# Two-layer encoder with routed experts on one core: the last gate matrix of each layer brought by eleven unequal transfers

## The reference, cut to what matters

```python
def block_fn(args):
    rows, e = args
    xb = x_pad[rows]
    h = jax.nn.silu(xb @ w_gate[e]) * (xb @ w_up[e])
    return h @ w_down[e]
```

## Time and profile before

| what | value |
|---|---|
| median of three runs | 1161.56 us (1160.43 to 1163.86) |
| the profiled execution's own time | 1162.22 us |
| its span, first to last instruction | 1160.4 us |
| time around the span | 1.8 us |
| busy share of the span: PE, PE weight loads, DVE, ACT, POOL | 76%, 44%, 20%, 15%, 4% |
| moved by DMA | 439.26 MB, 379 GB/s over the span |
| chain that ended last | PE 48%, DMA 45% |
| mean TensorE clock granted | 0.88 |

### The profile page before, as it was taken

How to read it: one execution, slowest core, us unless ns; L and a number is a source line. 1 busy time by engine, 2 the same in 40 slices (tenths; PEclk the granted TensorE clock), 3 DMA queues, 4 the chain that set the end, 5 groups by cost and what they waited for, 6 DMA issues and landing times.

```text
span 1160.4 us, 20228 instructions
## 1 busy us (share of the span) xinstructions
PE 879.7 (76%) x9135; PEld 510.6 (44%) x9135; DVE 237.3 (20%) x784; ACT 169.1 (15%) x459; POOL 41.5 (4%) x46
## 2 busy tenths in 40 slices
PE   9999995666576757566899999987575676666666
PEld 4454663434344434343544556644242443433343
DVE  2351421111012111110234435211110111111111
ACT  1141310101011101000224232211010110101011
POOL 1651000000000000000000000000000000000000
PEclk9999998879888887888999998988787787878789
DMA  9992999999999999999973258999999999999996
GB/s 347 336 324 99 380 428 425 429 425 429 426 428 426 426 429 424 429 426 425 393 292 118 100 227 353 383 424 429 426 428 426 426 428 425 430 425 427 426 426 271
DMA packets 46261, 439.26 MB, mean 379 GB/s; under 512 B 4640, under 2 KB 5888, under 8 KB 21344
## 3 DMA queue, kind: packets, MB, share of 16 engines
q1 hardware_dynamic: 43632, 433.96, 89.7%
q0 software_dynamic: 1088, 2.97, 1.1%
q10 hardware_dynamic: 1456, 1.04, 0.3%
HBM read 436.91 MB, written 1.05 MB: 377 GB/s over the span
## 4 chain that ended last, share of the span: by engine, by line
PE 48%; DMA 45%; another core or an unknown queue 2%; DVE 2%; ACT 1%; issue 1%; SPq 0%; POOL 0%; DVEq 0%
DMA mem<-in_moe_w_up 44%; PE psum L1311 43%; PE psum L1449 3%; PE psum L1441 1%; PE psum L1332 1%; DMA mem<-in_ev_w_in 1%; SPq L440 0%; DVE mem L962 0%; PE psum L1318 0%; ACT mem L645 0%; DVE mem L1112 0%; DVE mem L1108 0%; PE psum L1610 0%; PE psum L1376 0%
## 5 line engine op out<-in xcount | busy, mean ns | idle before, releaser
L1311 PE MATMUL psum<-mem 128*32 128x256 f32 (+3 forms) x7114 | 671.7, 438 | 258.8 <-DMA mem<-in_moe_w_up 226.2
L1311 PEld LDWEIGHTS psum<-mem 128*32 128x32 f32 (+2 forms) x7114 | 346.8, 132 | 554.9 <-issue 459.9
L1011 DVE TENSOR_TENSOR mem<-psum,mem 128x128 f32<-128x128 f32 x62 | 18.1, 291 | 645.6 <-ACT mem L659 645.6
L659 ACT ACTIVATE mem<-psum 128x128 f32<-128x128 f32 x62 | 17.2, 277 | 522.2 <-PE psum L1311 522.2
L1311 PE MATMUL psum<-mem,x 128*128 128x128 f32 (+1 forms) x576 | 71.5, 285 | 7.2 <-DVE mem L962 3.7
L1449 PE MATMUL psum<-mem 32*128 32x256 f32 x1024 | 73.3, 400 | 3.0 <-ACT mem L665 2.0
L1311 PEld LDWEIGHTS psum<-mem,x 128*128 128x128 f32 x576 | 69.5, 201 | 10.4 <-DVE mem L962 4.5
L1449 PEld LDWEIGHTS psum<-mem 32*128 32x128 f32 x1024 | 46.2, 184 | 30.7 <-issue 23.5
L970 DVE TENSOR_SCALAR mem<-cst,mem 128x128 f32<-128x128 f32 x124 | 37.2, 342 | 20.7 <-PE psum L1441 20.6
L665 ACT COPY mem<-psum 128x256 f32<-128x256 f32 x62 | 23.1, 372 | 95.2 <-PE psum L1311 95.2
L661 ACT COPY mem<-psum 128x256 f32<-128x256 f32 x62 | 23.1, 372 | 64.0 <-PE psum L1441 63.9
(11 more groups left out here) (168 smaller groups left out, 313.8 us busy)
## 6 DMA issues: line engine op xcount, KB each, us to landing
mem<-in_moe_w_gate SPq DMA_DIRECT2D x64, 2048.0 KB, 47.3
mem<-in_moe_w_up SPq DMA_DIRECT2D x64, 2048.0 KB, 48.0
mem<-in_moe_w_down SPq DMA_DIRECT2D x62, 2048.0 KB, 42.8
mem<-in_od_w_in SPq DMA_DIRECT2D x6, 2048.0 KB, 22.5
mem<-in_ev_w_in SPq DMA_DIRECT2D x3, 2048.0 KB, 19.4
mem<-in_ev_w_out SPq DMA_DIRECT2D x2, 2048.0 KB, 28.6
mem<-in_moe_w_down SPq DMA_DIRECT2D x4, 1024.0 KB, 41.9
mem<-in_od_w_out SPq DMA_DIRECT2D x2, 2048.0 KB, 20.0
```

The source lines that it names most:

```text
L659: nc.scalar.activation(M["sg"], bank(4)[:, 0:P], ACT.Silu).then_inc(s["silu"], 1)
L1011: link(V.tensor_tensor(M["h"], src, M["sg"], ALU.mult))
L1311: return nc.tensor.matmul(out_, lhsT, rhs, start=start, stop=stop)
```

## The change

Piece 93 of both expert phases, the gate matrix of the last place, is brought by eleven transfers in place of one. The first ten carry eight partitions each (0 to 7, 8 to 15, ... 72 to 79); such a transfer of eight rows is dealt to eight of the sixteen DMA engines, one row of 16 KB each. The eleventh carries the remaining 48 partitions (80 to 127), three rows for each of all sixteen engines. All eleven add 16 to the slot's semaphore, and the total that PE waits for is raised to match. Nothing else is moved: the waits before the piece, the slot, the bytes and the order of the queue stay.

```diff
+UNEVEN, EIGHTS = PIECES - 3, 10
...
-                total[n] += 16
+                total[n] += 16 * (EIGHTS + 1 if ph in RING and j == UNEVEN else 1)
                 arrived[ph, j] = (landed[n], total[n])
...
                 p, kind = divmod(n, 3)
+                if n == UNEVEN:
+                    rows = a["moe_w_gate"][l, p - 1].rearrange("(p r) f -> p (r f)", r=DC)
+                    for b in range(EIGHTS + 1):
+                        part = slice(8 * b, 8 * b + 8 if b < EIGHTS else P)
+                        sp.dma_start(piece_slot(ph, n)[part], rows[part]).then_inc(arrived[ph, n][0], 16)
+                    return
```

## The result

The changed kernel takes 1194.55 us (median of four runs, 1192.77 to 1197.79), the kernel before 1161.35 us beside it: the ratio is 1.0288, 95% interval 1.0261 to 1.0315, slower by 33.2 us. The forecast was 1183 us with a range to 1191; the result lies above the range, next to the sum of the rival "four in step" (1195.5). The profiled execution of after took 1197.79 us, 35.6 us more than that of before.

A forecast was written before the change was run, and what follows sets the result against it. The prediction took bytes in a full DMA queue to bound the expert phases; -3.0 us for shifted rows and 12.3 us a layer for colliding writes made +21.6 us, so 1183 us, range 1158 to 1191.

The forecast's parts named there:

- four in step: Rival for the eights' writes: four engines per port, factor 4, +33.9 us, 1195.5 us; inside the 0.63 for factors 2 to 4.
- The bound, the chain and the near one-for-one shift of the ends: Expert phases: full DMA queue sets the pace; a shift of up's last landings shifts the end nearly one for one.
- collision: Ten eights writing neighbouring partitions side by side: factor 3, 12.3 us more a layer; chance 0.63 for factors 2 to 4.
- rows on the engines that land last: Last landings in both layers: moving rows between engine halves gives -1.8 and -1.2 us, sum -3.0 us.
- the lead: Queue's end: one half of the engines finishes 4.9 us (layer 1) and 4.3 us (layer 0) before the other.
- the weight on the half behind: Rival at both layer ends: heavier half is the late one, +3.08 us a layer, +6.2 us; without collision 1167.7 us, chance 0.07.
- it works: Rival: writes don't collide and the heavier half is the one ahead; 1158.6 us, faster, chance 0.25.
- I stay near the row, above its 2, and take 3: Eights' slowdown factor: taken near the trace's bias transfers to 64 partitions at half rate; 3, or 12.3 us a layer.
- Up lands 4.9 us after gate, which covers 1.4 us: PE at the layer end: gate half slower after the longer wait, 1.4 us hidden before up lands.
- Ten more issues at no cost: SP's issue of the added transfers: 3.3 to 6.2 us, hidden before the issue of down; cost 0.
- What would show it: Signs in the profile: GB/s far below 426 at share near 1 or 0.5, gate waits some 10 us, eleven short issues.
- The range: Whole kernel: 1158 to 1191 us, to reach the second case and most of the first, whose own range was 1171 to 1195.

The follow-up runs named there:

- e9_leave_out: Against the changed kernel: piece 93 as one 128-row transfer of half columns plus eight every-fourth-partition eights, second half of rows 64 to 127 omitted; 1161.07 us, ratio 0.9999.
- e5_halves: Against the changed kernel: piece 93 in two transfers of 64 rows, no eights; 1184.28 us, ratio 1.0194 to the kernel before.
- e8_two_eights: Against the changed kernel: two eights in place of ten, the other 112 rows in one transfer; 1184.24 us, ratio 1.0193 to the kernel before.
- e6_columns: Against the changed kernel: piece 93 in eight transfers of all 128 rows, an eighth of the columns each; 1162.50 us, ratio 1.0004 to the kernel before.
- e7_step8: Against the changed kernel: eight eights, each of every eighth partition of 0 to 63, and one 64-row transfer; 1197.91 us, ratio 1.0311 to the kernel before.
- e1_near: Against the changed kernel: eight eights of neighbouring rows 0 to 63 and one 64-row transfer; 1193.68 us, ratio 1.028 to the kernel before.
- e2_spread: Against the changed kernel: eight eights, each of every fourth row within rows 0 to 63, and one 64-row transfer; 1182.28 us, ratio 1.0184 to the kernel before.

## Why the prediction was wrong

**What held.** The bound, the chain and the near one-for-one shift of the ends: each layer's loss went through to the end, 18.3 and 17.3 us, 35.6 in the profiled execution. That collision outweighs balance was right too.

The landings give the terms of the forecast's sum, both layers together and in the profiled execution:

| term | forecast, us | measured, us |
|---|---|---|
| rows on the engines that land last | -3.0 | +6.2 (estimate: 5 rows of 0.615 us more a layer) |
| collision | +24.6 (2 x 12.3) | +28.3: 14.9 in ordinary transfers ahead of gate, 13.4 in gate |
| PE behind the landings | 0 | +1.1 |
| sum | +21.6 | +35.6 |

The collision in gate is what its landing is later than that of the matrix before it, 8.7 and 10.9 us, less 3.1 us a layer for the rows.

**The step that failed is the lead:** "If the heavier half is the one ahead, it ends 3.08 us later and becomes the last: the landing of up moves by 3.08 - 4.9 = -1.8 us". The eights don't go to one half. Six of their engines are ahead and two are behind (e9_leave_out), and these two carry 13 rows in place of 8 and land last. So the term is +3.08 us a layer and not -1.8 and -1.2: 9.2 of the 14 us by which the forecast was short in the profiled execution (11 in the median). The forecast had +6.2 as its other bound, for "the weight on the half behind"; two engines are enough for it. The rival "it works" fails on this as well, before any collision.

**The collision has nearly the size forecast, but not its mechanism, and the nearness is luck.** "I stay near the row, above its 2, and take 3" puts 12.3 us a layer on the rows of the ten eights, and takes the 48-row transfer and all other engines as undisturbed. The engines that land last lost 7.5 and 7.4 us of a layer in ordinary transfers ahead of gate. In the slow stretches of the change (540 to 568 and 1150 to 1172 us) a packet of 16 KB took a median of 1.1 us, not quite twice 0.61, and none took over 2.1 us. And halves with no eight at all cost 23 us (e5_halves), and so does a transfer of 112 rows with two eights (e8_two_eights). By likeness with these, most of the collision goes with the last of the eleven transfers, the one with 48 rows, on which the prediction put no cost; no run has it alone. How the ten eights and it divide the 28.3 us stays open.

**The rival "four in step"** came within a microsecond of the median by errors that cancel. The rule of the Trainium skill, page "SBUF — State Buffer", section on the DMA port swizzle, which the prediction weighed beside its own, gave the factor 4 (by the forecast's own terms 16.7 to 17.3 us a layer, where the prediction has 16.5 to 17). The trace doesn't agree with it for these rows: four in step are 2.46 us a row, and the longest took 2.08. And the rival has the forecast's -3.0 us for the lead.

**Other steps.**

- *"Up lands 4.9 us after gate, which covers 1.4 us".* Gate decides now. From its landing to up's half PE took 5.97 us (1176.42 to 1182.39) at a granted clock of 0.50, the lower level of 1.2 GHz, after 9.83 us idle. Before it was 4.88 us, of which 1.48 were a wait for up. So PE was slower by 2.6 us and not 1.4; 1.1 us came through in D, and in B nothing, since the transposes behind it took less.
- *Ten more issues at no cost.* Right (e6_columns), though their length was not: 13.2 and 15.1 us for eleven against an estimate of 3.3 to 6.2 for ten.
- *What would show it.* GB/s far under 426 at a full share, and waits for gate of about 10 us (9.83 and 13.2), came as said. The late landings of other matrices weren't foreseen, and they are what tells a slow queue from a slow transfer.
- *The range.* It was cut at 1191 although the likeliest case's own range went to 1195 and a named rival stood at 1195.5. Leaving out the upper part kept the side of a gain to 1158, which had less for it.

**What stays open.** Why eights of every eighth row are as slow as neighbours (e7_step8). How rows are dealt to engines in a transfer of 64, 48 or 16 rows, engine by engine. Whether the reading side has a part in the cost of 64-row transfers. How the collision divides between the 48-row transfer and the eights: e1_near less e2_spread gives 11.4 us to neighbours, while e8_two_eights, which has eight eights fewer than the change, is only 10.3 us faster, 4.9 of them for four rows fewer on the last engines (estimate). That the instruction fetches cause the half's lag was argued from the earlier trace rows and wasn't tried. The increments fit it: the sixteen engines land a matrix within 0.5 us of one another at 120 us, 3.4 at 273 and 6.6 at 540, with a fetch every 15 us or so. No version here beat the kernel before.

## What to carry to other kernels

In a queue that is full, bring every matrix in transfers that have all 128 partitions, and if one must be split, split it by columns: here eight column parts cost nothing, two row halves 2%, and the loss was nearly the same in the middle of the stream as at its end. Before shifting load between engines, find out which engines are last, each by itself and not by halves, and which partitions each would write. Read the GB/s line beside the DMA share: a share of 1.0 at half the rate means packets that take twice as long, and the page's digit of 9 hides it.

## What was not expected of the hardware

- A transfer of fewer than 128 rows slows the other engines' ordinary transfers as well: 2.1 MB in two halves holds sixteen full engines at 197 to 238 GB/s for about 22 us, and every packet of 16 KB takes about 1.2 us in place of 0.61.
- Spread eights over partitions 0 to 63 are free (0.9999), and adding the same for 64 to 127 costs 16 us.
- The eight engines of an eight-row transfer were six of the half ahead and two of the half behind.
- Where an eight's rows lie in HBM made no difference (1195.64 and 1183.81, one execution each, follow the side that is written).
- A queue behind long transfers can hold SP for 31 us in seven issues without any loss of time.
